# Where the gate row is made at the start of a dense stage, and where one low part is made in the mixers' output stage

## The chip, the cores and the metric

One core of a Trainium2 chip runs the whole program in one launch. The metric is the device time of that launch in microseconds (us), the median of three runs. All data is in float32. The engines named below are TensorE (PE, matmuls), VectorE (DVE), ScalarE (ACT), GpSimd (POOL) and the queue of SyncE (SP), which issues the loads of weights.

## The reference, cut to what matters

A sequence of 256 tokens of width 1024 goes through two blocks of two layers each. A layer of the first block is a dense feed-forward part, a token mixer of three attentions, and a second dense feed-forward part. The second block has two attention layers, each followed by a mixture of 16 experts; the change does not touch it. Every part is normed and modulated before it and added to x behind it with a gate:

```python
def swiglu(h, w_gate, w_up, w_down):
    return (jax.nn.silu(h @ w_gate) * (h @ w_up)) @ w_down

def residual_add(x, y, g_post, gate, res_w):
    return x + res_w * (1 + gate) * rms_norm(y, g_post)

    for l in range(DEPTH):                       # DEPTH = 2
        ...
        h = modulate(x, norm_pre[l, 0], mod[:, 0, 0], mod[:, 0, 1])
        x = residual_add(x, swiglu(h, ...), norm_post[l, 0], mod[:, 0, 2], 0.5)
        ...
        y = token_mixer(h, ...)                  # ends in merged @ w_out
        x = residual_add(x, y, norm_post[l, 1], mod[:, 1, 2], 1.0)
        ...
        x = residual_add(x, swiglu(h, ...), norm_post[l, 2], mod[:, 2, 2], 0.5)
```

## The kernel before, in words

The program is one list of steps, made by `make_plan` and walked by every engine on its own; engines meet only at semaphores that count up. For each of the two layers of the first block the steps are norm, ffn (a dense stage), resid; norm, mixer, backT, out, resid; norm, ffn, resid. So there are four dense stages and two stages "out" (the product with `w_out`).

Weights come as one stream of chunks of 128 x 2048 numbers (1 MB). SP loads chunk n into one of six buffers (`stage`); it waits until the low part of chunk n-6 has been made. A float32 weight is used as the sum of two parts: ACT copies the chunk rounded to the matmul's format (`hi(n)`, L531, into `w_hi`), DVE subtracts that copy from the chunk (`lo(n)`, L991, into `w_lo`) and signals `chunk_ready`. There are three buffers for each part, so `hi(n)` waits until PE has used chunk n-3. Each product is three matmuls: high by high (L1760), low by high (L1763), high by low (L1764). One chunk makes 24 matmuls of 128 x 512.

The gate row: residual_add needs the gate of each of the 1024 columns on all 128 partitions. DVE writes eight diagonal blocks of factors (L1036, into the two halves of `tf`), PE multiplies them with a matrix of ones (L1812, two matmuls into the two banks of `tr`), and DVE copies the two banks to `tok` (L1043). Both engines have a function `gate_row` for it. DVE's has an argument `between`, a piece of work that is put between factors and copies; so far the stage of experts alone uses it.

A dense stage works on 11 blocks of 256 hidden columns. Block g has two up chunks (gate and up columns for the upper and the lower half of the input width) and a down chunk. PE's order is up, up for block 0, then the gate row, and then for g from 1: the first up chunk of block g, the transposes of the hidden block g-1, the second up chunk of block g, the down chunk of block g-1. The first up chunk of block g waits for `hid_ready` of block g-1: ACT takes silu of the gate columns (L597) when PE is through with the second up chunk, and DVE multiplies it with the up columns (L1130). ACT's order in a block is hi, silu, hi, hi, high part of the transposed hidden block; DVE's is lo, multiply (function `silu`), lo, lo, low part of the transposed block, with pieces of the modulation's product (`ada_add`, L1077 and L1079) between them from block 2 on. DVE goes through its `gate_row` before its block 1. What comes ahead of a dense stage on DVE is `take_lo` of the norm (L1009 and L1020), and PE's two first up chunks wait for its halves.

A stage "out" has four chunks (`rows`), and PE makes the gate row behind the second. DVE goes through `gate_row`, then `lo` of the third chunk and `lo` of the fourth. Ahead of it stands backT, which turns the merged mixers and splits them. `ahead` prepares the first two chunks of the next stage.

Of the kernel before, what the change touches and what calls it, by code (L numbers as in the profile page):

```python
# [255 lines left out]
def ffn_order(start, units):  # L256


    if not units:
        return (lambda g: start + 2 + g), None, 2  # L260
    return (lambda g: start + 2 + (g if g < 2 else 2 * g - 2)), (lambda g: start + 2 + 2 * g - 1), 4


def block_order(nb):


    peeled = 1 if nb % 2 == 0 else 2
    return peeled, (nb - 1 - peeled) // 2


def build(nc, wstream, ada_stream, xin, const_in, vec_in, bgate_in, lam_in, rbias_in, t5_in, rel_in, rw_in, out):
    plan = make_plan()
    n_chunks = plan[-1][1]["n"]
    dense_steps = [(step[1], b["n"]) for step, b in plan if step[0] == "ffn" and not step[3]]
    unit_base = {k: FIRST_UNITS + FFN_UNITS * i for i, (k, _) in enumerate(dense_steps)}

    assert FIRST_UNITS + FFN_UNITS * len(dense_steps) == UNITS and FFN_BLOCKS == FFN_UNITS + 2
    assert block_order(FFN_BLOCKS)[0] == 2

    with ExitStack() as ctx:  # L280
# [3 lines left out]
        def sem(name):  # L284
            return ctx.enter_context(nc.semaphore(name))
# [84 lines left out]
        tr_free = sem("tr_free")  # L370
# [153 lines left out]
        def _(act):  # L524
# [63 lines left out]
            def ffn(b, nb, units):  # L588
                peeled, turns = block_order(nb)
                n0, g0 = b["n"], b["hid"]  # L590
                u_of, _, per_turn = ffn_order(b["u"], units)

                def silu(g, i=0):
# [383 lines left out]
        def _(dve):  # L977
# [10 lines left out]
            def lo(n, i=0, rounds=1):  # L988

                dve.wait_ge(hi_ready, n + 1 + STAGES * rounds * i)  # L990
                dve.tensor_tensor(w_lo[:, n % PARTS, :], stage[:, n % STAGES, :], w_hi[:, n % PARTS, :].bitcast(F32),  # L991
                                  ALU.subtract).then_inc(chunk_ready, 1)
# [37 lines left out]
            def gate_row(b, k, u, between=None, tf0=None):  # L1030

                dve.wait_ge(tr_free, u + 2)
                tf0 = b["tf"] if tf0 is None else tf0
                for r in range(2):
                    for j in range(4):
                        ins = dve.tensor_scalar(tf[:, (tf0 + r) % 2, j * P:(j + 1) * P], ident,  # L1036
                                                mod[:, 3 * k + 2, 4 * r + j:4 * r + j + 1], None, ALU.mult)
                    ins.then_inc(tf_ready, 1)
                if between:
                    between()  # L1040
                for r in range(2):
                    dve.wait_ge(tr_full, u + r + 1)
                    dve.tensor_copy(tok[:, 0, r * 512:(r + 1) * 512], tr[:, (u + r) % 2, :]).then_inc(tr_free, 1)  # L1043
# [586 lines left out]
            for step, b in plan:  # L1630
# [51 lines left out]
                elif kind == "backT":  # L1682
                    take_lo(b, 4, hT_hi, hT_lo)
                elif kind == "out":
                    gate_row(b, step[1], b["u"])
                    lo(b["n"] + 2)
                    lo(b["n"] + 3)
                    ahead(b["n"] + 4)
                elif kind == "route":
# [57 lines left out]
                    u = b["u"] + 2  # L1747
# [9 lines left out]
        def _(pe):  # L1757
# [11 lines left out]
            def columns(n, dst, k0, kts, first, last, width=512, src=(hT_hi, hT_lo), i=0, pitch=512):  # L1769

                chunk_wait(n, i)
                s = n % PARTS
                for t in range(NT):
                    for k in range(kts):
                        c = slice(k * pitch, k * pitch + width)
                        lhs = [v[:, k0 + k, t * P:(t + 1) * P] for v in src]
                        ins = mm3(dst(t), lhs[0], lhs[1], w_hi[:, s, c], w_lo[:, s, c], first and k == 0, last and k == kts - 1)
                ins.then_inc(pe_used, 1)

            def rows(n, lhs, first, last, i=0, rounds=1):  # L1780

                chunk_wait(n, i, rounds)
                s = n % PARTS
                for t in range(NT):
                    for k in range(2):
                        l_hi, l_lo = lhs(k, t)
                        for h in range(2):
                            c = slice(k * D + h * 512, k * D + (h + 1) * 512)
                            ins = mm3(acc[:, 2 * t + h, :], l_hi, l_lo, w_hi[:, s, c], w_lo[:, s, c],
                                      first and k == 0, last and k == 1)  # L1790
                    if last and t == 0:
                        ins.then_inc(half_done, 1)
                ins.then_inc(pe_used, 1)

            def turn(u, srcs, i=0, per=0, scaled=None):


                if scaled is None:
                    pe.wait_ge(tr_free, u + 1 + per * i)
                else:  # L1800
                    pe.wait_ge(tf_ready, scaled)
                for j, src in enumerate(srcs):
                    rows_ = src.shape[-1]
                    ins = pe.transpose(tr[0:rows_, u % 2, j * P:(j + 1) * P], src, ident)  # L1804
                ins.then_inc(tr_full, 1)

            def gate_row(b, u, tf0=None):
                tf0 = b["tf"] if tf0 is None else tf0
                for r in range(2):
                    pe.wait_ge(tf_ready, tf0 + r + 1)  # L1810
                    pe.wait_ge(tr_free, u + r + 1)
                    pe.matmul(tr[:, (u + r) % 2, :], ones, tf[:, (tf0 + r) % 2, :], start=True,  # L1812
                              stop=True).then_inc(tr_full, 1)

            def ffn(b, nb, k=None):

                peeled, turns = block_order(nb)
                n0, g0 = b["n"], b["hid"]
                u_of, u_unit, per_turn = ffn_order(b["u"], k is not None)

                def up(n, half, g, i=0):
                    if half == 0:
                        pe.wait_ge(hid_ready, g0 + g + 2 * i)
                    columns(n, lambda t: gu[:, t, :], 4 * half, 4, half == 0, half == 1, i=i)

                def turn_hidden(g, i=0):
                    hid = pair[:, 1]
                    pe.wait_ge(hid_ready, g0 + g + 1 + 2 * i)
                    turn(u_of(g), [hid[:, t, c * P:(c + 1) * P] for c in range(2) for t in range(NT)], i, per_turn)

                def down(n, g, first=False, last=False, i=0):
                    pe.wait_ge(tr_free, u_of(g) + 1 + 2 + per_turn * i)
                    rows(n, lambda k, t: tuple(v[:, (2 * k + t) * P:(2 * k + t + 1) * P] for v in (hid_hi, hid_lo)),
                         first, last, i)

                def sum_unit(g, i=0):

                    unit, u = unit_base[k] + g - 2, u_unit(g)
                    pe.wait_ge(slice_sum, SLICES * (unit + 1) + 2 * SLICES * i)
                    pe.wait_ge(tr_free, u + 1 + per_turn * i)  # L1840
                    for j in range(UC):
                        ins = pe.matmul(tr[:, u % 2, j:j + 1], ada_acc[:, unit % 2, j * P:(j + 1) * P], ones[:, 0:1],  # L1842
                                        start=True, stop=True)
                    ins.then_inc(tr_full, 1)

                def block_(g, i=0):
                    up(n0 + 3 * g - 1, 0, g, i)
                    turn_hidden(g - 1, i)
                    if k is not None and g >= 3:
                        sum_unit(g - 1, i)  # L1850
                    up(n0 + 3 * g, 1, g, i)
                    down(n0 + 3 * g + 1, g - 1, isinstance(i, int) and g == 1, False, i)

                for half in range(2):
                    pe.wait_ge(tr_free, b["u"] + 2 * half)
                    up(n0 + half, half, 0)
                gate_row(b, b["u"])
                for g in range(1, 1 + peeled):
                    block_(g)
                with pe.Fori(0, turns) as i:  # L1860
                    block_(1 + peeled, i)
                    block_(2 + peeled, i)
                turn_hidden(nb - 1)
                if k is not None:
                    sum_unit(nb - 1)
                down(n0 + 3 * nb - 1, nb - 1, False, True)
# [505 lines left out]
            for step, b in plan:  # L2372
                kind = step[0]
                if kind == "norm":
                    pe.wait_ge(src_ready, b["src"] + 1)
                    for r in range(4):
                        u = b["u"] + r
# [4 lines left out]
                        ins.then_inc(tr_full, 1)  # L2382
                elif kind == "ffn" and not step[3]:
                    ffn(b, step[2], step[1])
                elif kind == "ffn":
                    l = (step[1] - 3 * DEPTH) // 2
# [23 lines left out]
                elif kind == "route":  # L2410
# [14 lines left out]
                    for j in range(8):  # L2425
                        part, t, half = j // 4, j // 2 % 2, j % 2
# [194 lines left out]
```

## Time and profile before

| | us |
|---|---|
| median of three runs | 2501.97 |
| the three runs | 2498.69 to 2506.42 |
| the profiled execution, its time | 2504.38 |
| the profiled execution, its span | 2502.6 |
| PE busy in the span | 2245.3 (90%) |
| DVE busy | 1473.1 (59%) |
| ACT busy | 880.8 (35%) |
| mean granted clock of PE | 0.953 of full speed |

The span is the stretch from the first to the last instruction of one execution; its own time lies 1.78 us above it. Matmuls run in a pipeline, so a matmul of 0.39 us starts each 0.23 us at full clock. A row of the timeline gives an instruction's start, its duration, and in brackets how long its engine had been idle before it and who ended that.

### The profile page before, as it was taken

What the parts mean: (1) busy time and instruction counts of PE and PEld (TensorE: products, weight loads), DVE (VectorE), ACT (ScalarE), POOL (GpSimd) and SP (SyncE); (2) the same over time, 40 slices, a digit from 0 to 9 for tenths busy, and PEclk for the clock granted to TensorE, in tenths of its full rate; (3) what the DMA queues carried; (4) which work ended last, traced back from release to release, by engine and by line L of the source; (5) the groups of instructions that cost most, each with busy time, mean ns of one, the idle gap of its engine ahead of it and who ended that gap; (6) DMA issues with size and microseconds to landing.
All of it is one profiled execution on the core that took longest, in us unless ns stands there. A gap on an engine that the chain in (4) does not pass through costs nothing.

```text
span 2502.6 us, 29929 instructions
## 1 busy us (share of the span) xinstructions
PE 2245.3 (90%) x10972; PEld 1688.1 (67%) x10972; DVE 1473.1 (59%) x2057; ACT 880.8 (35%) x1091; POOL 71.5 (3%) x93
## 2 busy tenths in 40 slices
PE   1899899987998999899987998976999979879998
PEld 1788788865887788788865887755555457645553
DVE  5688676745887688676746887674222147542212
ACT  1333455543333333455543333442111135211111
POOL 0000100000000000100000000110000001000000
PEclk9999999998999899999999999977899989879999
DMA  9588443324786588344324885420699964229997
GB/s 353 214 364 336 160 179 134 137 101 167 294 357 264 195 364 335 156 177 142 129 100 171 330 346 227 148 81 33 255 395 386 398 258 170 71 81 371 392 389 296
DMA packets 91804, 591.55 MB, mean 236 GB/s; under 512 B 10288, under 2 KB 13744, under 8 KB 36400
## 3 DMA queue, kind: packets, MB, share of 16 engines
q1 hardware_dynamic: 85520, 579.90, 59.8%
q10 hardware_dynamic: 6176, 10.15, 1.2%
q8 instruction: 75, 1.23, 0.2%
q14 instruction: 33, 0.27, 0.0%
HBM read 588.96 MB, written 1.05 MB: 236 GB/s over the span
## 4 chain that ended last, share of the span: by engine, by line
PE 84%; DVE 8%; ACT 3%; issue 2%; DMA 1%; POOL 1%; ACTq 0%; DVEq 0%; POOLq 0%
PE gu L2045 11%; PE acc L1760 11%; PE tr L2045 11%; PE acc L1763 10%; PE acc L1764 10%; PE gu L1760 7%; PE gu L1763 7%; PE gu L1764 7%; PE acc L2045 5%; PE tr L1804 3%; PE tr L1842 2%; DVE w_lo L991 1%; PE tr L1812 1%; DVE x_tok L1677 1%; DMA lam<-lam_in 1%
## 5 line engine op out<-in xcount | busy, mean ns | idle before, releaser
L991 DVE TENSOR_TENSOR w_lo<-stage,w_hi 128x2048 fp32r<-128x2048 f32 x240 | 547.5, 2287 | 102.2 <-ACT w_hi L531 102.1
L531 ACT ACTIVATE w_hi<-stage 128x2048 fp32r<-128x2048 f32 x240 | 457.2, 1910 | 296.3 <-PE acc L1764 273.7
L1760 PE MATMUL acc<-w_hi,hT_hi 128*128 128x512 f32 (+1 forms) x736 | 308.6, 419 | 15.2 <-DVE w_lo L991 6.1
L1760 PE MATMUL gu<-w_hi,hT_hi 128*128 128x512 f32 x704 | 281.5, 400 | 18.3 <-DVE pair L1130 14.3
L1079 DVE SCALAR_TENSOR_TENSOR qk<-proj,c_unit,qk 128x768 f32<-128x768 f32 x280 | 283.9, 1014 | 22.6 <-DMA proj<-ada_stream 11.8
L1763 PE MATMUL acc<-w_lo,hT_hi 128*128 128x512 f32 (+1 forms) x736 | 292.7, 398 | 0.0
L1764 PE MATMUL acc<-w_hi,hT_lo 128*128 128x512 f32 (+1 forms) x736 | 292.5, 397 | 0.0
L1763 PE MATMUL gu<-w_lo,hT_hi 128*128 128x512 f32 x704 | 277.7, 394 | 0.0
L1764 PE MATMUL gu<-w_hi,hT_lo 128*128 128x512 f32 x704 | 277.1, 394 | 0.0
L2045 PE MATMUL gu<-stage,got 128*64 128x512 f32 x1024 | 242.8, 607 | 1.6 <-DVE got L1199 1.6
L1760 PE MATMUL acc<-w_hi,yT_hi 128*128 128x512 f32 (+1 forms) x460 | 182.3, 396 | 9.0 <-DVE yT_lo L1559 5.7
L1760 PEld LDWEIGHTS acc<-w_hi,hT_hi 128*128 128x128 f32 x736 | 143.2, 195 | 55.4 <-issue 17.8
L1763 PE MATMUL acc<-w_lo,yT_hi 128*128 128x512 f32 (+1 forms) x460 | 180.1, 391 | 0.0
L1764 PE MATMUL acc<-w_hi,yT_lo 128*128 128x512 f32 (+1 forms) x460 | 180.0, 391 | 0.0
L1760 PEld LDWEIGHTS gu<-w_hi,hT_hi 128*128 128x128 f32 x704 | 134.3, 191 | 49.2 <-DVE pair L1130 17.6
L1764 PEld LDWEIGHTS acc<-w_hi,hT_lo 128*128 128x128 f32 x736 | 142.3, 193 | 30.9
L1763 PEld LDWEIGHTS acc<-w_lo,hT_hi 128*128 128x128 f32 x736 | 143.4, 195 | 26.0 <-issue 0.5
L1764 PEld LDWEIGHTS gu<-w_hi,hT_lo 128*128 128x128 f32 x704 | 134.2, 191 | 28.6
L1763 PEld LDWEIGHTS gu<-w_lo,hT_hi 128*128 128x128 f32 x704 | 133.9, 190 | 26.5
L2045 PEld LDWEIGHTS gu<-stage,got 128*64 128x64 f32 x1024 | 68.7, 138 | 122.5 <-issue 117.9
L635 ACT ACTIVATE pair<-gu 128x512 f32<-128x512 f32 x64 | 38.2, 598 | 287.6 <-PE gu L2045 287.6
L1220 DVE TENSOR_TENSOR hidT<-sgT,tr 128x256 f32<-128x256 f32 x32 | 13.5, 421 | 199.3 <-ACT sgT L640 199.3
(226 smaller groups left out, 2818.2 us busy)
## 6 DMA issues: line engine op xcount, KB each, us to landing
stage<-wstream SPq DMA_DIRECT2D x432, 1024.0 KB, 6.6
proj<-ada_stream SPq DMA_DIRECT2D x160, 768.0 KB, 7.6
tf<-bgate_in ACTq DMA_DIRECT2D x12, 256.0 KB, 4.5
proj<-rel_in ACTq DMA_DIRECT2D x16, 192.0 KB, 2.4
proj<-t_in ACTq DMA_DIRECT2D x8, 192.0 KB, 2.8
x_tok<-x_in ACTq DMA_DIRECT2D x1, 1024.0 KB, 14.4
x_out<-x_tok SPq DMA_DIRECT2D x1, 1024.0 KB, 4.0
const<-const_in ACTq DMA_DIRECT2D x1, 804.0 KB, 8.7
```

The lines of the kernel that those rows point to most:

```text
L531: act.activation(w_hi[:, n % PARTS, :], stage[:, n % STAGES, :], ACT.Copy).then_inc(hi_ready, 1)
L635: act.activation(both[:, j, :], gu[:, j, :], ACT.Copy).then_inc(both_ready, 1)
L991: dve.tensor_tensor(w_lo[:, n % PARTS, :], stage[:, n % STAGES, :], w_hi[:, n % PARTS, :].bitcast(F32), ALU.subtract).then_inc(chunk_ready, 1)
L1079: ins = dve.scalar_tensor_tensor(total, w, c, total, ALU.mult, ALU.add)
L1677: dve.tensor_tensor(x[:, t, :], x[:, t, :], tok[:, 1, :], ALU.add).then_inc(x_ready, 1)
L1760: ins = pe.matmul(dst, l_hi, r_hi, start=start, stop=False, skip_group_check=True)
L1763: pe.matmul(dst, l_hi, r_lo, start=False, stop=False, skip_group_check=True)
L1764: return pe.matmul(dst, l_lo, r_hi, start=False, stop=stop, skip_group_check=True)
L1804: ins = pe.transpose(tr[0:rows_, u % 2, j * P:(j + 1) * P], src, ident)
L1812: pe.matmul(tr[:, (u + r) % 2, :], ones, tf[:, (tf0 + r) % 2, :], start=True, stop=True).then_inc(tr_full, 1)
L1842: ins = pe.matmul(tr[:, u % 2, j:j + 1], ada_acc[:, unit % 2, j * P:(j + 1) * P], ones[:, 0:1], start=True, stop=True)
L2045: return pe.matmul(dst, lhs, rhs, start=start, stop=stop, skip_group_check=True)
```

## The change

In a dense stage PE makes the gate row between the two up chunks of block 0, not behind them. In the stage "out" DVE makes the low part of the third chunk between the factors and the copies of the gate row, not behind the copies. DVE's program in a dense stage and PE's program in the stage "out" are as they were.

```diff
@@ block.vector, the plan's loop
                 elif kind == "out":
-                    gate_row(b, step[1], b["u"])
-                    lo(b["n"] + 2)
+                    gate_row(b, step[1], b["u"], between=lambda: lo(b["n"] + 2))
                     lo(b["n"] + 3)
                     ahead(b["n"] + 4)
@@ block.tensor, ffn
-                for half in range(2):
-                    pe.wait_ge(tr_free, b["u"] + 2 * half)
-                    up(n0 + half, half, 0)
+                pe.wait_ge(tr_free, b["u"])
+                up(n0, 0, 0)
                 gate_row(b, b["u"])
+                up(n0 + 1, 1, 0)
                 for g in range(1, 1 + peeled):
                     block_(g)
```

## Rows read from the trace of the kernel before

**Rows 1.** The page, part 2: what the DMA engines moved, GB/s, in 40 slices.
```profile
GB/s 353 214 364 336 160 179 134 137 101 167 294 357 264 195 364 335 156 177 142 129 100 171 330 346 227 148 81 33 255 395 386 398 258 170 71 81 371 392 389 296
```

**Rows 2.** Waits, whole span: who waited <- for whom: us in total, times, longest.
```profile
PE gu L1760 <- DVE pair L1130: 14.3, 4, 3.6
```

**Rows 3.** Timeline of PE, start of the first dense stage: start, duration, line, tiles.
```profile
71.98 0.49 PE L1760 MATMUL gu<-w_hi,hT_hi 128*128 128x512 f32 x1 [1.15 <-DVE hT_lo L1009]
...
77.35 0.39 PE L1764 MATMUL gu<-w_hi,hT_lo 128*128 128x512 f32 x1
...
82.79 0.39 PE L1764 MATMUL gu<-w_hi,hT_lo 128*128 128x512 f32 x1
83.01 1.88 PE L1812 MATMUL tr<-tf,const 128*128 128x512 f32 x4
88.47 0.54 PE L1760 MATMUL gu<-w_hi,hT_hi 128*128 128x512 f32 x1 [3.58 <-DVE pair L1130]
```

**Rows 4.** Timeline of DVE in the same stretch.
```profile
74.46 1.67 DVE L1036 TENSOR_SCALAR tf<-const,mod 128x128 f32<-128x128 f32 x8
84.07 0.69 DVE L1043 COPY tok<-tr 128x512 f32<-128x512 f32 x1 [7.94 <-PE tr L1812]
...
85.54 2.28 DVE L991 TENSOR_TENSOR w_lo<-stage,w_hi 128x2048 fp32r<-128x2048 f32 x1
87.74 0.68 DVE L1130 TENSOR_TENSOR pair<-pair,gu 128x512 f32<-128x512 f32 x1
```

**Rows 5.** Timeline of ACT in the same stretch.
```profile
83.21 0.60 ACT L597 ACTIVATE pair<-gu 128x512 f32<-128x512 f32 x1 [6.40 <-PE gu L1764]
83.71 3.70 ACT L531 ACTIVATE w_hi<-stage 128x2048 fp32r<-128x2048 f32 x2
```

**Rows 6.** Line L1812 alone: durations in ns, shortest, median, longest.
```profile
L1812 PE MATMUL tr<-tf,const x40: 590/592/1222, 83.0 to 2223.5; 128*128 128x512 f32 x40
```

**Rows 7.** Timeline of PE, first stage "out", around its gate row.
```profile
566.13 1.88 PE L1812 MATMUL tr<-tf,const 128*128 128x512 f32 x4
571.08 0.77 PE L1760 MATMUL acc<-w_hi,hT_hi 128*128 128x512 f32 x1 [3.07 <-DVE w_lo L991]
```

**Rows 8.** Timeline of DVE in the same stage.
```profile
555.77 1.66 DVE L1036 TENSOR_SCALAR tf<-const,mod 128x128 f32<-128x128 f32 x8
...
568.05 0.69 DVE L1043 COPY tok<-tr 128x512 f32<-128x512 f32 x1 [0.17 <-PE tr L1812]
```

**Rows 9.** Timeline of ACT in the same stage.
```profile
554.91 1.91 ACT L531 ACTIVATE w_hi<-stage 128x2048 fp32r<-128x2048 f32 x1
560.95 1.92 ACT L531 ACTIVATE w_hi<-stage 128x2048 fp32r<-128x2048 f32 x1 [4.14 <-PE acc L1764]
```

**Rows 10.** Windows: stretch, its length, busy us (count) of five engines, PEclk, DMA, GB/s.
```profile
71.98:77.57 5.59, 5.58 (x24) 4.61 (x25) 3.95 (x12) 3.73 (x4) 0.00 (x0) 1.00 0.18 72
88.47:95.65 7.18, 7.18 (x25) 5.70 (x25) 4.35 (x2) 0.00 (x0) 0.00 (x0) 0.76 0.88 349
616.84:624.05 7.21, 7.21 (x25) 5.74 (x25) 4.35 (x2) 0.00 (x0) 0.00 (x0) 0.76 0.97 348
836.94:845.40 8.46, 8.46 (x24) 6.65 (x25) 4.35 (x2) 0.00 (x0) 0.00 (x0) 0.63 0.88 349
...
571.08:584.83 13.75, 13.75 (x48) 10.89 (x48) 6.64 (x4) 3.03 (x3) 1.03 (x2) 0.79 0.63 229
1318.96:1329.95 10.99, 10.99 (x48) 8.90 (x48) 6.65 (x4) 3.03 (x3) 1.03 (x2) 1.00 0.78 288
```

**Rows 11.** Timeline of PE: two shorter pauses in other stages.
```profile
1274.68 0.32 PE L2045 MATMUL acc<-proj,pair 128*128 128x64 f32 x1 [1.84 <-ACT pair L882]
...
1345.26 0.50 PE L1760 MATMUL gu<-w_hi,hT_hi 128*128 128x512 f32 x1 [1.15 <-DVE hT_lo L1009]
```

**Rows 12.** A window behind a pause of 1.84 us that ends at 525.18.
```profile
527.00:529.00 2.00, 2.00 (x6) 1.58 (x5) 0.00 (x0) 0.00 (x0) 0.00 (x0) 0.50 0.70 295
```

**Rows 13.** Waits of PE in the first dense stage, 60 to 280.
```profile
PE acc L1760 <- DVE yT_lo L1135: 0.2, 1, 0.2
```

## The prediction

> **What bounds the kernel now.** I read the page first, then the table of waits, then the timelines of PE, DVE and ACT at the places of the change, and last a table of windows. PE is busy for 90% of the span, so only pauses of PE, and the clock it runs at, are worth anything. In a dense stage PE runs through: between 60 and 280, behind the stage's first chunk and apart from the pause treated below, its waits on DVE come to one of 0.2 us [rows 13]. The table of waits shows the four pauses that the change is about: PE waits for `pair` from DVE four times, 14.3 us together, none above 3.6 [rows 2]. Each is the wait of block 1's first up chunk for the first hidden block.
>
> The timeline tells how such a pause comes about. PE starts the last matmul of the second up chunk at 82.79, makes the gate row from 83.01 on, and starts the next chunk at 88.47 behind 3.58 us of idleness [rows 3]. ACT has the silu done at 83.21 + 0.60 = 83.81 [rows 5]. DVE, however, stands in its gate row: it copies at 84.07 and once more behind that, makes `lo` at 85.54, and only then, at 87.74, multiplies [rows 4]. So the pause is gate row, two copies, one `lo` of 2.28 and the multiplication of 0.68, one after the other. In "out" it is the same without silu: the gate row begins at 566.13, the second copy at 568.05 [rows 8], and PE waits 3.07 us for `lo` of the third chunk [rows 7]; the second such stage shows the same 3.07.
>
> **Dense stage, part by part.** Nothing is added; the gate row's PE work is moved ahead of 24 matmuls. Its two matmuls are recorded as four passes of 0.59 [rows 6], in 1.88 from the first start to the last end [rows 3], so a pass starts each (1.88 - 0.59) / 3 = 0.43 and the row takes 1.72; with a slower first matmul behind it I take 1.80. The first up chunk's 24th matmul starts at 77.35 [rows 3], so the row can begin at 77.57. It needs DVE's factors, done at 74.46 + 1.67 = 76.13 [rows 4]: 1.4 us to spare, so PE does not wait there. The bound on the other side: if factors came late, PE would wait by as much, and DVE's later work would still have the whole second up chunk as cover.
>
> DVE's two copies then start some 1.06 behind the row's start, as now (84.07 - 83.01), at 78.6 and 79.5, and `lo` of chunk n0+2 runs from 80.1 to 82.4, all beside the second up chunk. It needs ACT's high part, which ACT makes ahead of the silu. What is left on the path behind the last up matmul (now at 82.79 + 1.80 = 84.59): 0.42 until ACT starts (83.21 - 82.79), silu 0.60, hand-over 0.05, multiplication 0.68, hand-over 0.05 (88.47 - 88.42) [rows 3 to 5]. PE goes on at 84.59 + 1.80 = 86.39, not at 88.47: 2.08 us earlier. The stretch from 83.01 to 87.74 that gate row, copies and `lo` fill now is not all gain: silu and multiplication are late next, and the gate row's 1.80 now delays them. A pause of 86.39 - 84.98 = 1.4 us stays. Four stages: 8.3 us.
>
> Does anything else come late? ACT's queue behind the silu shifts by 1.8: `hi` of n0+3 and n0+4, two in 3.70 [rows 5], end at 87.4 and 89.3. DVE's `lo` of n0+3 ends at 89.7 and PE wants it at 86.39 + 5.9 = 92.3; `lo` of n0+4 ends at 91.9, wanted at 97.8. On SP's queue the load of chunk n0+8, which waits for `lo` of n0+2, goes out some 5 us earlier, into a stretch where the DMA engines have been at 0.18 [rows 10]; the modulation's loads stand behind it in the queue and move with it. I cost both at nothing, with 2.6 us of cover.
>
> **Stage "out".** DVE's factors are done at 555.77 + 1.66 = 557.43 [rows 8]. ACT has the high part of the third chunk at 554.91 + 1.91 = 556.82 [rows 9], so `lo` runs from 557.5 to 559.8, long ahead of the copies at 567.19, which it doesn't delay. When PE is through with its gate row, at 566.13 + 1.72 = 567.85, the chunk is there: PE goes on at once, 3.2 us earlier than 571.08 [rows 7]. `lo` of the fourth chunk (high part done at 562.87 [rows 9]) follows the second copy, 568.66 to 570.9; PE wants it at 567.85 + 5.5 = 573.4. The cover is 2.4 us. The chunk load that `lo` lets go is 11 us earlier and finds free queues. Two stages: 6.4 us.
>
> Sum without the clock: 8.3 + 6.4 = 14.7 us.
>
> **The clock.** The table of windows shows that the pauses cost more than their length. The two last chunks of the second "out" are 48 matmuls at granted clock 1.00, in 10.99 us, so a chunk takes 5.55 from a standing start. The chunk behind the four dense pauses takes 7.18, 7.21, 8.46 and (the row left out) 7.20, at a mean granted clock of 0.76, 0.76, 0.63 and 0.76: 7.85 us too much, run partly at 1.2 GHz in place of 2.4. Behind the first "out" pause the two chunks take 13.75, 2.76 too much; behind the second nothing [rows 10]. In "out" no pause is left, so I take the whole 2.76. In the dense stages 1.4 us are left. The lower bound is nothing given back, as the clock fell to 0.50 behind a pause of 1.84 that ends at 525.18 [rows 12]. The upper bound is all 7.85: behind nine pauses of 1.07 to 1.84 (the first at 71.98 [rows 3], the eighth of 1.84 at 1274.68, the last at 1345.26 [rows 11]) the clock stayed up. 1.4 lies nearer to 1.15 than to 1.84, and even 1.84 lost only once in two; I take three stages of four, 5.9. Clock: 8.7 us.
>
> The same pause of 3.58 leaves one, 8.46, against three of about 7.2 [rows 10]. The Trainium skill, "TensorE: Matmul & The Clock Gate", Part 1, says the number of slow matmuls at a ramp varies from run to run and shouldn't be fitted. By it the clock term would be a draw, and the gain anything from 14.7 to 25.3; the trace agrees with it as far as the four dense stages go.
>
> **The sum.** 14.7 + 8.7 = 23.4 us off the profiled execution's 2504.38 gives 2481.0. That execution is 2.4 above the median of the runs, 2501.97, which gives 2478.6; I predict the median, 2478.6. Its own range is 2473 to 2484.
>
> **Rivals.** *The clock gives nothing back in the dense stages* (1.4 us of pause still lets it fall each time): 14.7 + 2.8 off, 2484.5, or 2487.3 if it falls in "out" too. For it: rows 12. Against it: the nine pauses of rows 11.
>
> *Another wait takes the place of the one removed.* In a dense stage `lo` of n0+3, in "out" `lo` of the fourth chunk would have to be over 2.4 us later than worked out; or the stage of experts, at 371 to 398 GB/s, would be held by the stream and take the gain back. Against the last: ahead of it the stream drops to 33 GB/s [rows 1], since its six buffers are full, so that stage starts from full buffers either way. If it holds, the time is 2495 to 2502.
>
> *Slower: the slow clock moves to where it is not now.* All behind the change shifts against whatever sets the clock. If our six places still lost what they lose (10.6), and the nine short pauses that now keep the clock lost 1.65 each, the least a dense pause loses, this takes 14.9 and the gain of 14.7 is gone: 2502.2; at 2.91 each it is 26.2, so 2513. It decides from 1.63 us a pause on, in all nine. For it: two like pauses of 1.84 differ in this very trace. Against it: eight of the nine are as short as 1.07 to 1.34.
>
> *The gate row stops PE between the two up chunks* in dense stages, because the factors come late. It would cost only what it lacks of 1.4 us of slack; a gain of 14.7 shrinks to nothing only when the wait is above 2 us in all four. I put it with the second rival.
>
> **Chances.** Forecast 0.62; no clock back in the dense stages 0.25; another wait or the gain absorbed 0.09; slower 0.04. 0.3%, 7.5 us, is about what a measurement of this kernel can tell from no change. Forecast and first rival are both beyond it: faster 0.90, within 0.07, slower 0.03. The range takes in the first rival, with some 3 us of scatter, as the three runs spread by 7.7: 2470 to 2490.
>
> **What would show it right or wrong.** In the timeline of PE, four rows of L1812 between two up chunks, and behind each second up chunk a pause of about 1.4 us on `pair` from DVE; in the table of waits that group falls from 14.3 to about 5.6. In "out" no pause behind L1812, and no wait of `acc` on `w_lo`. DVE's `lo` of n0+2 stands ahead of ACT's silu. The chunk behind the dense pause takes 5.6 us at clock 1.00 in three stages of four, and about 7.2 where the clock falls. Wrong would be: a pause ahead of L1812, pauses of the dense stages above 2 us, a wait on `w_lo` one chunk later, or equal stages and a longer stage of experts.

## The result, and the profile after

The changed kernel takes 2477.22 us (median of four runs, 2476.94 to 2477.32) against 2502.06 for the kernel before: 24.8 us less, ratio 0.9900, 95% interval 0.9882 to 0.9917. The forecast was 2478.6. The profiled execution has a span of 2475.1 us (2502.6 before) and a mean granted clock of 0.957 (0.953 before).

The waits of PE over the whole span, as in [rows 2] (who waited <- for whom: us in total, times, longest):

```profile
PE gu L1759 <- DVE pair L1130: 5.6, 4, 1.4
```

14.3 us have become 5.6, still in four pieces. Another group stood in the same table of the kernel before, the two pauses of "out":

```profile
PE acc L1760 <- DVE w_lo L991: 6.1, 2, 3.1
```

It is gone. How a dense stage starts now, in the timeline of PE, against [rows 3]:

```profile
71.88 0.50 PE L1759 MATMUL gu<-w_hi,hT_hi 128*128 128x512 f32 x1 [1.14 <-DVE hT_lo L1009]
...
77.49 1.88 PE L1811 MATMUL tr<-tf,const 128*128 128x512 f32 x4
78.81 0.79 PE L1759 MATMUL gu<-w_hi,hT_hi 128*128 128x512 f32 x1
...
84.47 0.39 PE L1763 MATMUL gu<-w_hi,hT_lo 128*128 128x512 f32 x1
86.27 0.50 PE L1759 MATMUL gu<-w_hi,hT_hi 128*128 128x512 f32 x1 [1.41 <-DVE pair L1130]
```

(PE's code stands one line higher: L1811 is L1812 of the kernel before.) The gate row stands between the up chunks and has no pause ahead of it. From the stage's first matmul to the first of block 1 it is 86.27 - 71.88 = 14.39 us, against 88.47 - 71.98 = 16.49 [rows 3]: 2.10 less. DVE and ACT in the same stretch, against [rows 4, 5]:

```profile
74.35 1.66 DVE L1036 TENSOR_SCALAR tf<-const,mod 128x128 f32<-128x128 f32 x8
78.55 0.69 DVE L1043 COPY tok<-tr 128x512 f32<-128x512 f32 x1 [2.53 <-PE tr L1811]
79.41 0.69 DVE L1043 COPY tok<-tr 128x512 f32<-128x512 f32 x1 [0.17 <-PE tr L1811]
80.02 2.28 DVE L991 TENSOR_TENSOR w_lo<-stage,w_hi 128x2048 fp32r<-128x2048 f32 x1
85.53 0.69 DVE L1130 TENSOR_TENSOR pair<-pair,gu 128x512 f32<-128x512 f32 x1 [3.23 <-ACT pair L597]
87.33 4.49 DVE L991 TENSOR_TENSOR w_lo<-stage,w_hi 128x2048 fp32r<-128x2048 f32 x2 [1.11 <-ACT w_hi L531]
```
```profile
84.90 0.60 ACT L597 ACTIVATE pair<-gu 128x512 f32<-128x512 f32 x1 [8.20 <-PE gu L1763]
85.39 3.71 ACT L531 ACTIVATE w_hi<-stage 128x2048 fp32r<-128x2048 f32 x2
```

Copies and `lo` lie beside the second up chunk. Behind it stand silu and multiplication alone: now DVE waits for ACT (3.23 us), while before the silu was done at 83.81 and DVE came to it only at 87.74 [rows 4, 5].

The first stage "out", timelines of PE and of DVE, against [rows 7, 8]:

```profile
560.93 1.88 PE L1811 MATMUL tr<-tf,const 128*128 128x512 f32 x4
562.24 0.79 PE L1759 MATMUL acc<-w_hi,hT_hi 128*128 128x512 f32 x1
...
573.35 0.39 PE L1763 MATMUL acc<-w_hi,hT_lo 128*128 128x512 f32 x1
```
```profile
551.56 1.66 DVE L1036 TENSOR_SCALAR tf<-const,mod 128x128 f32<-128x128 f32 x8
553.13 2.29 DVE L991 TENSOR_TENSOR w_lo<-stage,w_hi 128x2048 fp32r<-128x2048 f32 x1
561.98 0.69 DVE L1043 COPY tok<-tr 128x512 f32<-128x512 f32 x1 [6.57 <-PE tr L1811]
...
563.45 4.48 DVE L991 TENSOR_TENSOR w_lo<-stage,w_hi 128x2048 fp32r<-128x2048 f32 x2
```

PE has no pause in brackets behind the gate row. The windows from the gate row's start to the start of the stage's last matmul show both stages, first of the kernel before and then of the changed one. A row gives the stretch, its length, the busy us (and count) of PE, PEld (the weight loads of PE), DVE, ACT and POOL, then PE's granted clock, the DMA engines' busy share and GB/s:

```profile
566.13:584.60 18.47, 15.40 (x53) 11.48 (x51) 10.27 (x6) 4.94 (x4) 1.01 (x2) 0.82 0.47 170
1314.01:1329.72 15.71, 12.64 (x53) 9.50 (x51) 10.28 (x6) 4.94 (x4) 1.01 (x2) 1.00 0.54 201
```
```profile
560.93:573.35 12.42, 12.42 (x53) 9.58 (x51) 8.07 (x5) 4.95 (x4) 1.01 (x2) 1.00 0.46 169
1294.59:1307.01 12.42, 12.42 (x52) 9.59 (x51) 8.08 (x5) 4.94 (x4) 1.01 (x2) 1.00 0.46 170
```

The first stage gained 6.05 us, the second 3.29.

The windows of the chunk behind the four dense pauses, against [rows 10]:

```profile
86.27:91.87 5.60, 5.60 (x25) 4.57 (x25) 4.49 (x2) 2.83 (x2) 0.00 (x0) 1.00 0.23 63
603.50:609.10 5.60, 5.60 (x24) 4.57 (x25) 4.49 (x2) 2.83 (x2) 0.00 (x0) 1.00 0.21 48
819.85:825.47 5.62, 5.62 (x25) 4.57 (x26) 4.50 (x2) 2.83 (x2) 0.00 (x0) 1.00 0.24 58
1337.12:1342.74 5.62, 5.62 (x24) 4.57 (x25) 4.50 (x2) 2.83 (x2) 0.00 (x0) 1.00 0.27 58
```

All four are at granted clock 1.00 and take 5.6 us in place of 7.2 to 8.5.

The two profiled executions can be split at the norm behind each stage. The table gives the stretches in us; their sum is the difference of the two spans.

| stretch | before | after | less |
|---|---|---|---|
| start to the first norm's matmuls | 64.95 | 64.71 | 0.24 |
| the four dense stages, each to the next norm | 219.92, 220.09, 221.34, 219.83 | 216.37, 216.40, 216.36, 216.38 | 15.67 |
| the two mixers with backT and "out" | 308.33, 303.68 | 300.85, 300.90 | 10.26 |
| both attention layers with experts | 944.46 | 943.13 | 1.33 |
| span | 2502.6 | 2475.1 | 27.5 |

Four stages that took 219.8 to 221.3 now take 216.4 within 0.04. The spans differ by 27.5 us and the medians by 24.8, since the profiled execution of the kernel before (2504.38) lay 2.3 above its median.

### The profile page after: what moved, and what is told of

Its sections match the earlier page's. It is cut to its first block, busy times and chain, and to the rows that moved or that the text cites. A ratio compares the mean times of both kernels' runs of the same rounds, so it can differ in the third digit from the quotient of the medians.

```text
span 2475.1 us, 29925 instructions
## 1 busy us (share of the span) xinstructions
PE 2234.0 (90%) x10972; PEld 1680.7 (68%) x10972; DVE 1473.7 (60%) x2057; ACT 880.7 (36%) x1091; POOL 71.5 (3%) x93
## 4 chain that ended last, share of the span: by engine, by line
PE 85%; DVE 8%; ACT 3%; issue 2%; DMA 1%; POOL 1%; ACTq 0%; DVEq 0%; POOLq 0%
PE gu L2044 11%; PE acc L1759 11%; PE tr L2044 11%; PE acc L1763 11%; PE acc L1762 11%; PE gu L1759 7%; PE gu L1762 7%; PE gu L1763 7%; PE acc L2044 5%; PE tr L1803 3%; PE tr L1841 2%; DVE w_lo L991 1%; PE tr L1811 1%; DVE x_tok L1677 1%; DMA lam<-lam_in 1%
## 5 line engine op out<-in xcount | busy, mean ns | idle before, releaser
L2044 PE MATMUL tr<-tok,x_tok 128*128 128x128 f32 x320 | 62.3, 381 | 77.7 <-DVE tok L1640 77.3
```

What stands on the lines that cost most here:

```text
L2044: return pe.matmul(dst, lhs, rhs, start=start, stop=stop, skip_group_check=True)
```

## The experiments

**One edit at a time.** First the dense stage alone: the diff shown above for PE, with DVE's "out" left as it was.

> Only the dense edit: the gate row between the two up chunks of block 0, 'out' as before. Theory A (the moved gate row takes 2.1 us out of each of four pauses, and the clock no longer falls behind the 1.4 us that stay): 8.3 + 7.4 = 15.7 us off, some 2486 us; PE's wait on pair is 1.4 us four times, the chunk behind it takes 5.5 to 5.6 us at granted clock 1.00. Rival B (the clock's fall has nothing to do with the length of the pause, and the gain seen with both edits came from elsewhere): 8.3 us off, 2494 us, with the chunk behind the pause still at 7.2 in some stages. The pause of 3.07 us in both 'out' stages must be there again.

Then "out" alone:

> Only the edit in 'out': low part of the third chunk between factors and copies, dense stages as before. Theory A: 6.4 us of pause and up to 2.8 of clock off, 2493 to 2496 us; the four pauses of 3.58 stay in the dense stages and each is followed by a chunk of 7 to 8.5 us. The two single edits' gains add up to the 24.8 us of both within the scatter of 3 us. Rival B (the edits help each other, since one stage's earlier end changes what the next finds): the sum of the single gains is below 20 us.

Measured, beside the kernel before on one chip at 2503.74: the dense edit 2486.7 (ratio 0.9929, 0.9912 to 0.9945), the "out" edit 2493.88 (0.9958, 0.9942 to 0.9975). That is 17.0 and 9.9 us, 26.9 together, where both at once gave 24.8 on their chip and 29.2 on another (below). The gains add up; neither edit needs the other. The dense edit was expected to give 15.7 and gave 17.0. In its profiled execution the four dense stages are 15.8 us shorter than in the kernel before, of 18.2 between the two spans; the rest lies in stretches that this edit does not touch. PE's waits for DVE in the dense edit alone, then in "out" alone:

```profile
PE acc L1760 <- DVE w_lo L991: 6.1, 2, 3.1
PE gu L1760 <- DVE pair L1130: 5.6, 4, 1.4
```
```profile
PE gu L1759 <- DVE pair L1130: 14.3, 4, 3.6
```

Each edit removes its own wait and leaves the other's. With "out" alone the chunk behind the four dense pauses still takes 7.18, 7.19, 8.16 and 8.09 us; the 17.0 of the dense edit is about twice the 4 x 2.1 of its pauses. Rival B fell in both.

In the dense edit alone both pauses of "out" are there as before, 3.07 us each, but the windows from the gate row to the last matmul are not those of the kernel before. It had 18.47 and 15.71 us; here it is 17.32 and 17.35, the first of them:

```profile
559.73:577.05 17.32, 14.24 (x53) 10.64 (x51) 10.28 (x6) 4.94 (x4) 1.01 (x2) 0.90 0.47 182
```

So what a pause of 3.07 us in "out" costs beyond its length differs between executions of the same code: 2.8, nothing, 1.6 and 1.6 us so far.

**Is it the pause that costs the clock?** The kernel before gets work of no use in its dense pause:

```diff
                 gate_row(b, b["u"])
+                for _ in range(12):
+                    pe.matmul(acc[:, 0, :], hT_hi[:, 0, 0:P], hT_hi[:, 0:2, :].rearrange("p a s -> p (a s)"),
+                              start=True, stop=True, skip_group_check=True)
                 for g in range(1, 1 + peeled):
```

> The kernel before (neither edit), with 12 matmuls of 128 x 512 added on PE behind the gate row of each dense stage; they write a PSUM bank that is cleared afterwards, so the pause of 3.58 us on pair is cut to about 0.8 by work that is of no use, and the next chunk can't start any sooner. Theory A (the pause itself lets the clock fall): the chunk behind it runs at full clock, 5.5 us in place of 7.2 to 8.5, and the kernel is 7 to 8 us faster than before with more work in it, 2496 us. Rival B (the slow chunk is slow for another reason: loads, a new stage, the low parts of DVE beside it): the chunks still take 7.2 or more and the time is that of before, within 3 us.

Measured: 2491.9 us (2491.34 to 2498.84) against 2503.29, ratio 0.9965 (0.9951 to 0.9979). A kernel with 48 matmuls more is 11.4 us faster by the medians, and 5 to 12 us by the interval; 7 to 8 were expected. Its timeline of PE, and windows of the first and the third of the four chunks:

```profile
84.06 3.33 PE L1859 MATMUL acc<-hT_hi 128*128 128x512 f32 x12
88.21 0.50 PE L1760 MATMUL gu<-w_hi,hT_hi 128*128 128x512 f32 x1 [0.81 <-DVE pair L1130]
```
```profile
88.21:93.83 5.62, 5.62 (x24) 4.56 (x25) 4.34 (x2) 0.00 (x0) 0.00 (x0) 1.00 0.88 325
...
830.37:835.99 5.62, 5.62 (x24) 4.57 (x25) 4.35 (x2) 0.00 (x0) 0.00 (x0) 1.00 0.89 322
```

The second and the fourth take 5.60, also at 1.00. The next chunk starts as late as before (23.6 us behind the norm's first matmul, 23.5 before), the DMA engines are nearly as full as before (0.88, where [rows 10] have 0.88 to 0.97), DVE makes its two low parts beside it as before, and the clock stays up. So neither loads nor low parts nor the new stage were the cause. Between norms its dense stages take 218.3 to 218.5 us, 7.7 less in all, as theory A had it: that is what the filled pauses gave. The two profiled spans differ by 12.6 us, and the other 4.9 lie in stretches that this edit does not touch. 2.8 of them are in the first "out": its pause of 3.07 us stands as before, but the clock stays up behind it this time, and its window is 15.69 us and not 18.47:

```profile
564.24:579.93 15.69, 12.62 (x53) 9.50 (x51) 10.27 (x6) 4.94 (x4) 1.01 (x2) 1.00 0.51 201
```

**How long may a pause be?** In the changed kernel the first multiplication waits behind useless ones, each half its size:

```diff
                     dve.wait_ge(sg_ready, g0 + g + 1 + 2 * i)
+                    for _ in range({0: 1, 2: 2, 3: 3, 5: 4}[k] if isinstance(i, int) and g == 0 else 0):
+                        own(dve.tensor_tensor(hid[:, 0], sg[:, 0], gu[:, 0, BLK:2 * BLK], ALU.mult))
```

> The changed kernel, with 1, 2, 3 and 4 useless multiplications of 128 x 256 ahead of the first hidden block's in the four dense stages in this order, so that the pause of PE is some 1.9, 2.3, 2.8 and 3.2 us in place of 1.41. Theory A: from some length on the chunk behind the pause takes 7 us or more at a lower mean clock; at 1.9 it is likely still 5.6, at 3.2 it is 7.2. Time 2477 + 4.6 for the pauses + up to 7.4 for the clock, 2482 to 2489 us. Rival B: all four chunks take 5.6 us, 2482 us.

> As the run with rising pauses, but 4, 3, 2 and 1 multiplications in the four stages. If it is the length of the pause that decides, the slow chunks stand now in the first stages; if it is the stage, they stand where they stood; if chance decides at lengths between 1.9 and 3.2, the two runs disagree on a length. Time as there, 2482 to 2489 us.

Measured: 2487.95 (2 runs) and 2488.45 us (2 runs), both at the upper end of what was expected. The windows of the four chunks, behind pauses of 1.86, 2.32, 2.77 and 3.23 in the first kernel, and of 3.23, 2.77, 2.32 and 1.86 in the second:

```profile
87.02:94.19 7.17, 7.17 (x25) 5.69 (x25) 4.49 (x2) 2.37 (x2) 0.00 (x0) 0.76 0.43 155
607.93:615.14 7.21, 7.21 (x24) 5.71 (x25) 4.49 (x2) 1.92 (x2) 0.00 (x0) 0.76 0.47 172
826.98:834.19 7.21, 7.21 (x25) 5.69 (x25) 4.35 (x2) 1.46 (x1) 0.00 (x0) 0.76 0.54 187
1347.54:1355.92 8.38, 8.38 (x24) 6.63 (x25) 4.35 (x2) 1.00 (x1) 0.00 (x0) 0.64 0.62 230
```
```profile
88.03:95.02 6.99, 6.99 (x25) 5.62 (x26) 4.35 (x2) 1.00 (x1) 0.00 (x0) 0.78 0.52 184
609.03:616.24 7.21, 7.21 (x24) 5.70 (x25) 4.35 (x2) 1.47 (x1) 0.00 (x0) 0.76 0.54 201
827.91:835.11 7.20, 7.20 (x24) 5.70 (x25) 4.49 (x2) 1.92 (x2) 0.00 (x0) 0.76 0.51 181
1348.60:1354.17 5.57, 5.57 (x24) 4.57 (x25) 4.49 (x2) 2.37 (x2) 0.00 (x0) 1.00 0.27 81
```

All six pauses from 2.32 up made a chunk of 7 us or more, in whichever stage they stood. At 1.86 one did and one did not. I had expected 1.86 to be harmless. These two stood in different stages, so they alone do not tell a draw from an effect of the stage; the table does it for a like pause elsewhere. It counts, over the twelve profiled executions of this document (before, changed, and the ten experiments), how often the granted clock was at its lower level, 0.50, within 2 us of the pause's end. Besides the dense stages it has every other place with a pause of 1.3 to 3.6 us, from the first dense stage to the last:

| pause of PE, us | where | clock at 0.50 |
|---|---|---|
| 0.81 | dense, pause filled | 0 of 4 |
| 1.38 and 1.41 | dense, `lo` out of the way | 0 of 20 |
| 1.86 | dense, lengthened | 1 of 2 |
| 2.32, 2.77, 3.23 | dense, lengthened | 6 of 6 |
| 3.58 | dense, as before | 8 of 8 |
| 3.07 | "out", as before | 3 of 6 |
| 1.34 | start of the mixer | 0 of 24 |
| 1.83 | end of the mixer, on ACT's `pair` | 15 of 24 |
| 2.83 | end of the mixer, on `yT_lo` | 24 of 24 |
| 1.51 | backT, first | 0 of 24 |
| 1.71 | backT, second, 1.1 us of work behind the first | 11 of 24 |

As far as these runs tell, it is thus a draw whether the clock falls behind a pause of 1.8 us. In the dense stage 1.41 was on the safe side of it each time; nothing was measured there between 1.41 and 1.86. Length alone does not decide, though: the 3.07 us of "out" slowed PE in half of the cases, and the 1.71 of backT, close behind a pause of 1.51, slowed it in 11 of 24. This is the first 1.71 of the kernel before, and the window behind it:

```profile
552.66 1.71 PE L1804 MATMUL tr<-const,tok 128*128 128x128 f32 x8 [1.71 <-DVE hT_lo L1009]
```
```profile
552.66:556.00 3.34, 3.34 (x13) 2.79 (x14) 2.16 (x5) 2.18 (x3) 0.00 (x0) 0.55 0.80 282
```

What else decides is not shown.

**Is it the place of the gate row?** PE's order as before, and in the dense stage DVE makes `lo(n0 + 2)` between factors and copies, as the change does in "out":

```diff
                     add(0)
-                    lo(n0 + 3 * g - 1, i)
+                    if not isinstance(i, int) or g > 1:
+                        lo(n0 + 3 * g - 1, i)
...
-                gate_row(b, k, b["u"])
+                gate_row(b, k, b["u"], between=lambda: lo(n0 + 2))
```

> 'out' as in the changed kernel; in the dense stage PE's order is that of before (gate row behind both up chunks), and DVE makes the low part of chunk n0+2 between factors and copies. The theory that the gain in the dense stage is DVE's low part, not the place of the gate row: PE starts its gate row at once behind the second up chunk, DVE copies at +1.1 and +1.9 and multiplies at +2.6 us, the next chunk starts some 1.4 us behind the gate row's end, as in the changed kernel, so the time is that of the changed kernel, 2477 us within 3. The rival that PE's order itself matters (the gate row has to stand between the up chunks): the pause stays above 3 us and the time is near 2493.

> DVE's low part between factors and copies, PE's order as before, on the same chip as the changed kernel. The theory that the low part and not the place of the gate row is what pays: within 3 us of the changed kernel. Rival: it keeps the 4 us by which its first median stood better against the kernel before.

The changed kernel itself ran on that chip too:

> The changed kernel itself, beside the two variants of the dense start on one chip, so that the three can be compared without the difference between chips. 24 to 27 us below the kernel before.

Measured: PE's old order took 2475.02 us at first (0.9880, 0.9863 to 0.9896), and 2476.65 (0.9891, 0.9875 to 0.9908) on one chip with the changed kernel, which took 2474.76 (0.9886, 0.9869 to 0.9902). These two are 1.9 us apart, with intervals that overlap. The changed kernel is 29.2 us below the kernel before on this chip, more than the 24 to 27 that were expected of it. In its profiled execution the dense stages take the same 216.2 to 216.4 as in the first one; the mixers take about 2 us less.

With PE's old order the pause is 1.38 us and the four chunks take 5.6 at clock 1.00. Its start in the first dense stage:

```profile
83.08 0.39 PE L1764 MATMUL gu<-w_hi,hT_lo 128*128 128x512 f32 x1
83.31 1.88 PE L1812 MATMUL tr<-tf,const 128*128 128x512 f32 x4
86.56 0.50 PE L1760 MATMUL gu<-w_hi,hT_hi 128*128 128x512 f32 x1 [1.38 <-DVE pair L1130]
```

PE's order is thus one of two ways to the same thing. What had to leave the path is DVE's low part. With it gone, it is 3.48 us from the last up matmul to the next chunk, gate row and copies included (86.56 - 83.08). In the changed kernel it is 1.80, and 1.76 more for the gate row between the chunks: 3.56.

**A better one.** If the low part and the first multiplication both come between factors and copies, and PE keeps its old order, the gate row can fill the pause:

```diff
                     add(1)
-                    silu(g - 1, i)
+                    if not isinstance(i, int) or g > 1:
+                        silu(g - 1, i)
...
-                gate_row(b, k, b["u"])
+                gate_row(b, k, b["u"], between=lambda: (lo(n0 + 2), silu(0)))
```

(`lo` of block 1 is left out as in the variant before.)

> 'out' as in the changed kernel; in the dense stage PE's order is that of before, and DVE makes the low part of chunk n0+2 and also the first multiplication (pair) between factors and copies. PE's gate row then runs while ACT and DVE finish the first hidden block: silu ends 1.02 us behind the start of the last up matmul, the multiplication 0.73 later, the gate row's passes 1.94 later. Theory A: PE goes on at once behind the gate row, no pause of pair is left, the dense start is 1.5 us shorter than in the changed kernel in each of four stages: 6 us, so 2471 us. Rival: the copies, which now come 2 us later, or the low part of n0+3 behind them, make a new pause in the same chunk, and the time stays at 2477 or goes above.

> Low part and first multiplication between factors and copies, PE's gate row in the pause, on the same chip as the changed kernel: 1.5 us less in each of four dense stages, 5 to 7 us below the changed kernel.

Measured: 2469.14 us at first (0.9856, 0.9839 to 0.9872), and 2466.84 (0.9856, 0.9840 to 0.9872) beside the changed kernel's 2474.76: 7.9 us below it, where 5 to 7 were expected. The timelines of PE and DVE in the first run:

```profile
83.32 1.88 PE L1813 MATMUL tr<-tf,const 128*128 128x512 f32 x4
84.89 0.54 PE L1761 MATMUL gu<-w_hi,hT_hi 128*128 128x512 f32 x1
```
```profile
84.15 0.69 DVE L1130 TENSOR_TENSOR pair<-pair,gu 128x512 f32<-128x512 f32 x1 [5.50 <-ACT pair L597]
84.75 1.28 DVE L1043 COPY tok<-tr 128x512 f32<-128x512 f32 x2
85.95 4.49 DVE L991 TENSOR_TENSOR w_lo<-stage,w_hi 128x2048 fp32r<-128x2048 f32 x2
```

No pause stands behind the gate row, and the late copies hold up nobody. The next chunk starts 1.80 us behind the last up matmul (at 83.09), where the changed kernel has 1.80 and 1.76 for the gate row besides. So the gate row has left the path whole, 1.76 us a stage and not the 1.5 of the expectation. A dense stage takes 214.6 us from norm to norm, 1.8 less than in the changed kernel, 7.1 for the four; on the chip they shared it is 7.3, of 9.4 between the two spans. This version beats both kernels.

## Why the prediction was right

*What bounds.* PE alone. All that was taken from PE's pauses came out at the end; the stage of experts took nothing back (943.13 against 944.46).

*Dense stage.* The start of the stage was to be 2.08 us shorter and is 2.10; a pause of 1.4 was to stay, and 1.41 stays. The gate row between the chunks was put at 1.80. The last up matmul starts 84.47 - 77.49 = 6.98 us behind the gate row's start, against 82.79 - 77.57 = 5.22 for the same 24 matmuls before, so it costs 1.76. The factors were 1.48 us early for the gate row (76.01 against 77.49), as worked out. `lo` of n0+3 was made from 87.33, forecast 87.4.

*"Out".* Forecast were 3.2 us of pause a stage, and 3.29 came out in the second stage, where the clock had no part. `lo` of the third chunk began at once behind the factors, and that of the fourth behind the copies, with no pause on PE. Pauses together: 8.4 in the dense stages and 6.6 in "out" are 15.0, forecast 14.7.

*Clock.* The mechanism held, and the filled pause shows it; the size of the term was in part luck. The forecast was 5.9 + 2.8 = 8.7, and 10.0 came out. In the dense stages I gave one stage in four back to the slow clock, and none went there, nor any in the 20 stages with a pause of 1.38 or 1.41. The stages gave 15.67, of which 8.4 is pause, so the clock gave 7.3 and not 5.9. The four chunks themselves became 7.6 us shorter, not the 7.85 at stake in the prediction, since a chunk behind a pause takes 5.6 at full clock and not 5.55. In "out" the clock gave 6.05 - 3.29 = 2.76, as forecast, but that is against one trace of the kernel before. The same pause of 3.07 us lost 2.8 us there, nothing in the second stage, 1.6 twice in the dense edit alone and nothing twice in the filled kernel. For both stages of one execution that is 2.8, 3.2 and 0 us.

*What the prediction left out.* It counted nine pauses of 1.07 to 1.84 behind which the clock stayed up, and one of 1.84 behind which it fell. Two of 1.71, each close behind one of 1.51 in backT, stand in the same trace with the clock down behind both. They are nearer to 1.41 than the 1.84 that it took as its bound. They spoke for the first rival; as it turned out, they tell nothing of a single pause of 1.41.

*Sum.* 9.34 in "out" and 15.67 in dense stages make 25.0 of the 27.5 us between the two spans; the other 2.5 lie in stretches that the change does not touch. The forecast was 23.4, and the medians moved by 24.8 here and by 29.2 on the other chip. Such untouched stretches differ by a few us between executions, so that the forecast time was met within 1.4 us (2478.6 against 2477.22) is partly luck.

*Slow clock elsewhere.* The rival was that slow stretches move to other pauses, and make the kernel slower. A little of the first is there. The end of the second mixer, from the same pause on (1.84 us before [rows 11], 1.82 after), in windows of before and of after:

```profile
1274.68:1290.00 15.32, 11.31 (x48) 8.99 (x49) 3.76 (x7) 6.47 (x6) 0.00 (x0) 0.89 0.20 68
```
```profile
1255.08:1270.40 15.32, 11.30 (x41) 8.72 (x42) 2.66 (x6) 6.47 (x6) 0.00 (x0) 0.78 0.18 68
```

The same length holds 48 matmul records in one and 41 in the other. The second mixer layer with "out" gained 2.78 where its "out" gave 3.29, so some 0.5 was lost there; the first gained 7.48 with 6.05 in "out", 1.4 more. These draws came out at 0.9 us less in sum. Of the nine short pauses that the rival counted only this one, of 1.82, has the clock down behind it in the changed kernel.

*The other rivals.* No clock back (2484.5), another wait, and the gate row stopping PE: none is in the trace. PE's table of waits has no group that it did not have before.

## What to carry to other kernels

When a wait on a helper engine ends a pause, look at what stands ahead of the wanted instruction in that engine's order. Here a low part of 2.28 us and two copies could be elsewhere, and only silu and multiplication had to be in the pause. Price the pause together with the chunk behind it, and do it from more than one execution. In the dense stages a pause of 2.3 us or more cost 1.4 to 2.9 us more in slow matmuls each time, about as much as the edit took out of the pause itself, and one of 1.4 cost nothing; in "out" one of 3.07 cost 1.6 to 2.8 in three of six cases and nothing in the others. If PE has work that nobody waits for at once, as this gate row, the pause is a good place for it: that was worth another 7 to 8 us.

## What the runs showed of the hardware

48 matmuls of no use, put into four pauses of 3.58 us so that 0.81 was left, took 7.7 us out of the four stages, with the pauses' ends and the DMA load as before. The granted clock of the chunk behind was 1.00 in all four, against 0.63 to 0.76: 2.4 GHz throughout against a part at 1.2. Over twelve profiled executions single pauses of up to 1.51 us were never followed by the lower clock in the places counted above, and those of 1.82 to 1.86 were in 16 of 26 cases. Those of 2.3 to 3.6 were in 38 of 38 cases outside "out", where the pause of 3.07 was in 3 of 6.
